# Reading the moving operand in alternating token blocks, and rotating four PSUM banks instead of two

## What is computed

```python
q = einsum('bld,dk->blk', x, wq)                  # queries, 8 heads x 2 halves
s = einsum('blhpc,hpnc->blhpn', q, sub_keys)      # scores against 128 keys each
s1, i1 = top_k(s[..., 0, :], 16); s2, i2 = top_k(s[..., 1, :], 16)
top_s, pos = top_k(s1[..., :, None] + s2[..., None, :], 16)   # 16 experts a head
g = softmax(top_s)
h = x @ u[e].T            # hidden values; u is 16384 x 2048
y = (g * gelu(h)) @ v[e]  # v is 16384 x 2048
```

## Time and profile before

| | |
|---|---|
| median of 3 runs | 3672.01 us |
| profiled execution, its own time | 3675.29 us |
| its span | 3673.4 us |
| PE busy | 3656.2 us (100%) |
| DVE, ACT, POOL busy | 2468.2 (67%), 1900.6 (52%), 975.3 us (27%) |
| mean granted TensorE clock | 0.999 |
| U stage of the first layer | 452.64 to about 1168 us |
| U stage of the second layer | about 2283 to 2998 us |

### The profile page before, as it was taken

How to read it: one execution, slowest core, us unless ns; L and a number is a source line. 1 busy time by engine, 2 the same in 40 slices (tenths; PEclk the granted TensorE clock), 3 DMA queues, 4 the chain that set the end, 5 groups by cost and what they waited for, 6 DMA issues and landing times.

```text
span 3673.4 us, 58215 instructions
## 1 busy us (share of the span) xinstructions
PE 3656.2 (100%) x19252; PEld 3188.1 (87%) x19252; DVE 2468.2 (67%) x4281; ACT 1900.6 (52%) x2859; POOL 975.3 (27%) x557
## 2 busy tenths in 40 slices
PE   9999999999999999999999999999999999999999
PEld 8888888888888888888888888888888888888888
DVE  6766599985555566665687666999855556656666
ACT  4675455554444444444456754555544454444443
POOL 1000038777770000000011000477777600000000
PEclk9999999999999999999999999999999999999999
DMA  8765567777776777777667555677777777777774
GB/s 302 247 219 201 201 206 210 216 207 217 207 215 252 261 256 251 251 255 254 223 235 248 196 197 207 207 208 217 212 213 208 216 263 251 255 255 251 252 256 177
DMA packets 294652, 842.44 MB, mean 229 GB/s; under 512 B 98832, under 2 KB 198672, under 8 KB 210192
## 3 DMA queue, kind: packets, MB, share of 16 engines
q1 hardware_dynamic: 183952, 807.30, 62.9%
q0 software_dynamic: 73728, 0.29, 4.4%
q10 hardware_dynamic: 36864, 33.57, 2.9%
HBM read 771.57 MB, written 69.47 MB: 229 GB/s over the span
## 4 chain that ended last, share of the span: by engine, by line
PE 97%; DVE 1%; ACT 1%; issue 0%; DMA 0%; SPq 0%; DVEq 0%; ACTq 0%
PE bank L475 28%; PE bank L477 14%; PE bank L706 12%; PE bank L708 12%; PE bank L707 12%; PE bank L489 5%; PE bank L491 5%; PE bank L490 5%; PE bank L517 1%; PE bank L530 1%; PE bank L546 1%; PE bank L502 0%; PE bank L675 0%; ACT scr L839 0%; DMA arena<-x_t_in 0%
## 5 line engine op out<-in xcount | busy, mean ns | idle before, releaser
L1147 DVE TENSOR_TENSOR lo<-raw,hi 128x1024 fp32r<-128x1024 f32 x1288 | 1582.3, 1230 | 937.3 <-ACT hi L766 928.7
L766 ACT ACTIVATE hi<-raw 128x1024 fp32r<-128x1024 f32 x1288 | 1359.8, 1057 | 1340.1 <-PE bank L708 682.5
L475 PE MATMUL bank<-xhl,hi 128*128 128x512 f32 x4480 | 1146.7, 393 | 0.0
L1113 POOL DMA_INDIRECT gates_scratch<-sel,slots x512 | 913.1, 1783 | 854.4 <-issue 479.9
L475 PEld LDWEIGHTS bank<-xhl,hi 128*128 128x128 f32 x4480 | 795.3, 189 | 131.8
L706 PE MATMUL bank<-hi,xhl 128*128 128x512 f32 x2016 | 764.4, 379 | 1.4 <-DVE xhl L1623 1.2
L707 PE MATMUL bank<-lo,xhl 128*128 128x512 f32 x2016 | 764.1, 379 | 0.0
L708 PE MATMUL bank<-hi,xhl 128*128 128x512 f32 x2016 | 764.1, 379 | 0.0
L477 PEld LDWEIGHTS bank<-xhl,lo 128*128 128x128 f32 x4480 | 630.9, 190 | 57.0
L477 PE MATMUL bank<-xhl,lo 128*128 128x256 f32 x4480 | 646.6, 282 | 0.0
L706 PEld LDWEIGHTS bank<-hi,xhl 128*128 128x128 f32 x2016 | 381.0, 189 | 56.5 <-DVE lo L1147 1.9
(11 more groups left out here) (179 smaller groups left out, 2141.3 us busy)
## 6 DMA issues: line engine op xcount, KB each, us to landing
raw<-u_t SPq DMA_DIRECT2D x256, 1024.0 KB, 5.0
raw<-v_t SPq DMA_DIRECT2D x256, 1024.0 KB, 4.8
raw<-w_in SPq DMA_DIRECT2D x76, 1024.0 KB, 6.4
gates_scratch<-arena SPq DMA_DIRECT2D x32, 1024.0 KB, 8.4
raw<-w_out SPq DMA_DIRECT2D x32, 1024.0 KB, 4.9
raw<-wq SPq DMA_DIRECT2D x32, 1024.0 KB, 4.8
gelu_scratch<-gelu_out ACTq DMA_DIRECT2D x256, 128.0 KB, 4.1
scr<-gelu_scratch SPq DMA_DIRECT2D x256, 128.0 KB, 4.6
```

What stands on the lines that cost most here:

```text
L475: pe.matmul(acc[:], w, xhl[:, c, :, :].rearrange("p a t -> p (a t)"), start=(c == 0), stop=False)
L766: act.activation(to[:], half, ACT.Copy).then_inc(hi_done, 1)
L1113: pool.indirect_dma_start(out=gate_dram[layer].rearrange("i p t -> (i p t)").unsqueeze(1), out_offset=bass.IndirectOffsetOnAxis(ap=slots[: ...
L1147: dve.tensor_tensor(wide_lo[v][:], half, wide_hi[v][:].bitcast(F32), ALU.subtract).then_inc(lo_done, 1)
```

## The change

Three edits. The moving operand of `both_parts` is read with the two blocks of 128 tokens in turn (token 0, 128, 1, 129, ...) where it was read straight, so the columns of a bank now stand in that order; whoever reads a bank (`store_q_group`, `take_cross`, `sum_q_group`, `add_cross`) takes every second column (`by_block`) and writes the tokens in their old order (`in_blocks`). The U tiles rotate over banks 0 to 3 where they rotated over banks 0 and 1, and a tile waits for the sum four tiles back where it waited for two back. The 36 matmuls at the end are gone.

```diff
+def by_block(cols):
+    return cols.rearrange("p (t b) -> p b t", b=NB)
+
+def in_blocks(cols):
+    return cols.rearrange("p (b t) -> p b t", b=NB)
...
 def both_parts(acc, wh, wl, chunks):
     for c, w in zip(chunks, wh):
-        pe.matmul(acc[:], w, xhl[:, c, :, :].rearrange("p a t -> p (a t)"), start=(c == 0), stop=False)
+        pe.matmul(acc[:], w, xhl[:, c, :, :].rearrange("p a (b t) -> p a t b", b=NB), start=(c == 0), stop=False)
     for c, w in zip(chunks, wl):
-        last = pe.matmul(acc[:, L:2 * L], w, xh[:, c, :], start=False, stop=(c == DC - 1))
+        last = pe.matmul(acc[:, L:2 * L], w, xh[:, c, :].rearrange("p (b t) -> p t b", b=NB), start=False,
+                         stop=(c == DC - 1))
...
 def hidden(i, j, first=False):
     pe.wait_ge(lo_done, i * BODY + (AT_U + j + 1))
     if j % 2 == 0 and not first:
-        pe.wait_ge(summed, i * NRAW + (j // 2 - 1))
-    h = bank[j // 2 % 2]
+        pe.wait_ge(summed, i * NRAW + (j // 2 + 1 - NRAW))
+    h = bank[j // 2]
...
 for j in range(BODY):
-    pe.wait_ge(keys_stored, 1 if j < 2 else 2 if j < 4 else 8)
-    hidden(0, j, first=j < 4)
+    pe.wait_ge(keys_stored, j // 2 + 1)
+    hidden(0, j, first=True)
+pe.wait_ge(keys_stored, 8)
...
 def store_q_group(g):                       # ACT
-    act.activation(q_t[:, 4 * g + j, :], bank[4 * (g % 2) + j][:, L:2 * L], ACT.Copy)
+    act.activation(in_blocks(q_t[:, 4 * g + j, :]), by_block(bank[4 * (g % 2) + j][:, L:2 * L]), ACT.Copy)
 def take_cross(i, m, rounds, first=False):  # ACT
-    act.activation(gelu_out[m % 2][:], bank[m % 2][:, L:2 * L], ACT.Copy)
+    act.activation(in_blocks(gelu_out[m % 2][:]), by_block(bank[m][:, L:2 * L]), ACT.Copy)
 def sum_q_group(g):                         # DVE
-    dve.tensor_tensor(q_t[:, 4 * g + j, :], bank[4 * (g % 2) + j][:, 0:L], q_t[:, 4 * g + j, :], ALU.add)
+    total = in_blocks(q_t[:, 4 * g + j, :])
+    dve.tensor_tensor(total, by_block(bank[4 * (g % 2) + j][:, 0:L]), total, ALU.add)
 def add_cross(i, m):                        # DVE
-    dve.tensor_tensor(gelu_out[m % 2][:], bank[m % 2][:, 0:L], gelu_out[m % 2][:], ALU.add)
+    total = in_blocks(gelu_out[m % 2][:])
+    dve.tensor_tensor(total, by_block(bank[m][:, 0:L]), total, ALU.add)
...
-for m in moving:                            # PE, beside the last layer norm
-    for _ in range(4):
-        pe.matmul(bank[0][:, 0:int(np.prod(m.shape[1:]))], xh[:, 0, 0:P], m, start=True, stop=True)
```

More of the change, by code:

```diff
@@ L867, in store_q_group @@
                         for j in range(4):
-                            act.activation(q_t[:, 4 * g + j, :], bank[4 * (g % 2) + j][:, L:2 * L], ACT.Copy).then_inc(q_stored, 1)
+                            act.activation(in_blocks(q_t[:, 4 * g + j, :]), by_block(bank[4 * (g % 2) + j][:, L:2 * L]), ACT.Copy).then_inc(q_stored, 1)
                     def root(k, b):
@@ L1020, in take_cross @@
                             act.wait_ge(gelu_stored[m % 2], rounds * 16)
-                        act.activation(gelu_out[m % 2][:], bank[m % 2][:, L:2 * L], ACT.Copy).then_inc(crossed, 1)
+                        act.activation(in_blocks(gelu_out[m % 2][:]), by_block(bank[m][:, L:2 * L]), ACT.Copy).then_inc(crossed, 1)
                     def gelu(i, m):
@@ L1466, in sum_q_group @@
                             dve.wait_ge(q_stored, 4 * (g - 1) + j + 1)
-                            dve.tensor_tensor(q_t[:, 4 * g + j, :], bank[4 * (g % 2) + j][:, 0:L], q_t[:, 4 * g + j, :],
-                                              ALU.add).then_inc(q_summed, 1)
+                            total = in_blocks(q_t[:, 4 * g + j, :])
+                            dve.tensor_tensor(total, by_block(bank[4 * (g % 2) + j][:, 0:L]), total, ALU.add).then_inc(q_summed, 1)
                     def add_cross(i, m):
                         dve.wait_ge(crossed, i * NRAW + (m + 1))
-                        dve.tensor_tensor(gelu_out[m % 2][:], bank[m % 2][:, 0:L], gelu_out[m % 2][:], ALU.add).then_inc(summed, 1)
+                        total = in_blocks(gelu_out[m % 2][:])
+                        dve.tensor_tensor(total, by_block(bank[m][:, 0:L]), total, ALU.add).then_inc(summed, 1)
                     def query_low(j):
@@ L1676, in columns @@
                 return x[:, b, q * W:(q + 1) * W]
[L1678 to L1684, removed]
-                          xhl[:, 0:9:8, 0, :].rearrange("p c t -> p t c"),
-                          xhl[:, 0:9:8, :, 0:P].rearrange("p c a t -> p a t c"),
-                          xhl[:, 0:2, 0, 0:P].rearrange("p c t -> p t c"),
-                          xhl[:, 0:2, 0, :], xhl[:, 0, 0, 0:P]]
-                for m in moving:
-                    for _ in range(4):
-                        pe.matmul(bank[0][:, 0:int(np.prod(m.shape[1:]))], xh[:, 0, 0:P], m, start=True, stop=True)
             @block.scalar
```

## The result

The changed kernel takes 3621.81 us (median of 3 runs, 3619.23 to 3622.3) against 3672.01 before: 0.986 of the time, interval [0.9837, 0.9882]. That is 50.2 us saved; the forecast was 77. The time lies in the range of 3580 to 3630 us and 27 us above the forecast.

A forecast was written before the change was run, and what follows sets the result against it. PE was taken to bound the kernel, with DVE setting the pace in the routing. Per layer 12.4 + 22.0 + 4.2 = 38.6 us, 77.2 for two; 3675.3 - 77.2 = 3598.1, less 3.3 for the profiled execution: 3595 us, range 3580 to 3630.

The forecast's parts named there:

- 256-column case: Rival: in U halves the 256-column matmuls keep their 0.119 us, so 3613 us; chance 0.08.
- strided reads that cost DVE time: Rival: reading every second bank column costs DVE 0.26 us more each in the routing, so 3628 us; chance 0.08.
- the scatter: POOL's scatter before V: ends near 1098, v about 3 us late against 12 us in hand; counted as nothing.
- The read pattern: U and query halves: 512-column matmuls at 0.2156 us, 256-column at 0.1115, a half 2.617 us, 0.176 less.
- The routing: U stage to half 131: DVE's pace decides, so 12.4 us a layer saved there, not 23.
- DVE's 6.9 us of waits: DVE's waits for ACT's high part in the routing, excluding one of 7.4 us: all its slack in 16 bodies.
- PE's 5.5 us in hand: Before the change, half 131's low part is done 5.5 us before PE starts that half; the faster PE uses this up.
- Some 10.7 us a layer: New PE waiting for DVE's low part by half 131, at the end of the routing: some 10.7 us a layer.
- Four banks: U tiles rotating over four banks: counted 0, at most 2 us a layer hidden behind DVE's pace.
- the end: Removing the 36 matmuls at the kernel's end: 0, since DVE's chain there outlasts them untouched.
- slower, by the clock: Rival: small PE idle pieces in the routing make the clock fall, one per tile giving 3889 us; chance 0.03.
- SP waiting long for the scatter: Sign named in advance, before the V stage, that would show the forecast wrong; no size given.

The follow-up runs named there:

- straight_four_banks: The kernel before with only the four banks and their waits added, operand and banks still read straight: 3672.52 us, ratio 1.0.
- extra_matmul: The changed kernel with one more unread 512-column matmul per U half from the ninth on, slowing PE to about its old pace: 3683.17 us, ratio 1.0028.
- one_input_low: The changed kernel with each U half's low-part subtraction replaced by an 8-column one and a one-input MAX8 over 1024 columns: 3617.5 us, ratio 0.9849.
- turns_two_banks: The changed kernel with the alternating read, but the old two banks and the wait for the sum two tiles back: 3623.33 us, ratio 0.9868.
- end_matmuls_kept: The changed kernel with the 36 unread matmuls put back beside the last layer norm: 3619.16 us, ratio 0.9854.

## Why the prediction was right and where it was wrong

**The range was met in part by luck.** Its upper end of 3630 us was there for the 256-column case and for strided reads that cost DVE time, and neither came. What moved the time to 3622 is the scatter, a term put at nothing, for which the range had no room of its own. From the sum to the result: 3598.1 + 23.9 for the seam + 2.4 for small shortfalls in the other stages - 2.6 of drift = 3621.8, the profiled execution, which is here the median. The forecast was another 3.3 us lower because the profiled execution of before lay above its median.

**The read pattern: right.** 0.216 and 0.111 us against 0.2156 and 0.1115, and a half at 2.62 against 2.617. That the 256-column matmuls gain too was settled by them; straight_four_banks puts the whole gain on the pattern. The Trainium skill, "TensorE: Matmul & The Clock Gate", section "Back-to-back issue gap", has one spacing per column count in its table of isolated gaps; this case's rows agree with it, within 0.003 us, for reads by turns only.

**The routing: right in mechanism and size.** Forecast 12.4 us up to half 131, measured 11.7 and 11.6. The reasoning (DVE's 6.9 us of waits are all that it can give, PE's 5.5 us in hand are used up) holds: one edit that shortens the low part brought 22.7, another that makes DVE's work for a half 0.08 us longer brought 2.7. "Some 10.7 us a layer" of PE waiting was right as a delay (11.5); the view of waits shows half of it.

**Four banks, strided reads, the end: right.** 0 was counted for each; at most 1.2 us a layer, 425 against 425 ns, and nothing came out. The clock stayed at 1.00 in the routing, though PE idled 5.6 of the 250 us from 550 to 800:

```profile
550.00:800.00 250.00, 244.44 (x1462) 221.55 (x1461) 236.31 (x593) 136.23 (x198) 195.10 (x100) 1.00 0.75 216
```

That was the rival "slower, by the clock". The warning that stood at it (the Trainium skill, "TensorE: Matmul & The Clock Gate", section "A second HAM failure mode: psum-queue depth-cycling": a clock that oscillates with banks taken in turn and small idle pieces) did not come true here.

**The scatter: wrong.** The step was "POOL only about 6 (its start follows the first routed heads). POOL ends near 1098 ... Nothing". Its first half came out even better: the first scatter of layer 1 starts 8.7 us earlier. The unspoken half failed, that the 256 scatters then take as long as before. They take 614.9 us, not 591.8, so POOL ends 14.4 us later, not 4 to 6 earlier, and v's first tile is some 20 us late rather than 3, against the 12 us in hand. The margin was seen, and "SP waiting long for the scatter" was named as a sign that would show it wrong; what I did not do was put a price on the wait beyond the margin, or a rival. A look at the rows that I had would have warned: the mean of 1783 ns over a 1.55 us scatter said that some scatters take longer, and asking which ones leads to the low parts, whose rhythm the change was bound to alter.

What the runs show of the cause: the long scatters are there with either number of banks, fall from 55 to 14 of 128 when PE's pace is put back (extra_matmul; 12 before the change), and are gone when the low part's second SBUF input is gone (one_input_low). What links scatter and low part inside the chip no run here shows directly. The Trainium skill, "SBUF — State Buffer", section "SBUF: two separate sides", describes it: a DVE instruction with two SBUF inputs and a GpSimd operation that reads SBUF use one shared port pair, and the one that comes second is blocked until the first ends. The trace agrees on the side of the scatter: a held one ends 1.41 to 1.43 us behind the low part, so all but about 0.13 us of its 1.55 us comes after the low part's end. The other way round it does not: 76 low parts of the changed kernel start during a scatter between 860 and 1100 us, and the longest takes 1.24 us.

The same traces hold another pair in which both sides wait: POOL's additions with two SBUF inputs in the attention mixer (lines 1111 to 1117), and the low parts beside them. First a low part that starts during an addition, then an addition that starts during a low part:

```profile
210.10 1.29 POOL L1111 TENSOR_TENSOR scr<-scr 128x512 f32<-128x512 f32 x1 [23.21 <-DVE scr L1202]
211.04 1.43 DVE L1159 TENSOR_TENSOR lo<-raw,hi 128x1024 fp32r<-128x1024 f32 x1
...
181.73 1.22 DVE L1159 TENSOR_TENSOR lo<-raw,hi 128x1024 fp32r<-128x1024 f32 x1
181.89 2.18 POOL L1111 TENSOR_TENSOR scr<-scr 128x512 f32<-128x512 f32 x1 [21.76 <-DVE scr L1202]
```

The first low part ends at 212.47, 1.08 us behind the addition's end; all 16 low parts of this trace that start inside such an addition of POOL do so and take 1.42 to 2.19 us in place of 1.23. The second addition ends 1.12 us behind the low part and takes 2.18 us in place of 1.29. So the instruction that starts second does nearly all of its work after the first has ended, whichever engine it is on, and a scatter can be that second one but, as the 76 low parts show, holds up no low part itself.

**The consequence of that wait: larger than the idle time.** 8 to 9 us of idle time on PE also took the clock down to 1.2 GHz, 4.6 and 2.3 us more, so that 17 us of idle time cost 23.9. I had weighed the clock for many small gaps and not for one long one at the seam.

What stays open: why a scatter waits for a low part but holds up none; and what sets the cost of the clock's fall. It is no matter of the layer: in turns_two_banks it is 1.9 us in layer 1 and 3.1 in layer 2, behind 9.4 and 7.25 us of idle time, and in end_matmuls_kept 2.3 and 2.2, behind 8.0 and 9.4.

## What to carry to other kernels

- When the bound engine gets faster, list who is next by the waits that each has left, and then the engines that are off the path: not only how much slack they have, but whether their pace hangs on the rhythm of the engine that is sped up. A mean above an operation's shortest time is the sign to look for.
- A wait in an in-order queue delays all that stands behind it. Put loads that don't need the awaited result ahead of it; here that alone was worth 23 us, and with it the lateness of the scatter did no harm.
- Read the pace of pipelined matmuls from their starts, and try the order in which the moving operand is read where the output allows it: it was worth 6% of these matmuls' time, and the reads of the banks got no dearer.

## What the runs showed of the hardware beyond that

- An indirect scatter of POOL takes 1.55 us alone. When it starts while DVE runs a low part (two SBUF inputs, 1.23 us) it takes up to 2.59 us, the longer the earlier it starts; beside a one-input operation of the same length it stays at 1.55 (mean 1551 ns of 512). Low parts and POOL's two-input additions hold each other up in the same way, 1.23 and 1.29 us becoming up to 2.2.
- Elementwise operations that read every second column of a bank and write in runs are as fast as straight ones: 425 ns against 425 for DVE and 385 against 384 for ACT at 256 columns.
- Behind an idle time of 8.3 us on PE the granted clock was 0.50 for 8.2 us, with matmuls 0.43 us apart, and 1.00 before; 5.6 us of small gaps in 250 us left it at 1.00.
